# Sample attention of a decoder step: fresh keys turned once, second values loaded early, later value rows issued by ScalarE

## The reference

```python
kv_ext = jnp.concatenate([zeros(w), buf, kv_new], axis=1)
idx = q_idx[:, None] - offs[None, :]
logits = einsum('bhtd,btnhd->bhtn', q, kg) * HEAD_DIM ** -0.5 + bias
p = exp(logits - max); o = einsum('bhtn,btnhd->bthd', p / sum(p), vg)
```

## Time and profile before

| what | value |
|---|---|
| median of 3 runs | 2270.28 us (2265.86 to 2270.36) |
| profiled execution, its own time | 2268.59 us |
| span of the profiled execution | 2266.8 us |
| mean granted TensorE clock | 0.992 of full |
| DMA | 305.62 MB, mean 135 GB/s |
| attention stage in the span | about 1660 to 1828 us |

### The profile page before, as it was taken

One profiled execution on the slowest core, in us unless ns is written; L12 is line 12 of the kernel. 1 busy time (PEld: TensorE's weight loads), 2 busy tenths in 40 slices (PEclk: granted clock), 3 DMA queues, 4 the chain that ended last, 5 costly groups with the idle time before them and its releaser, 6 DMA issues.

```text
span 2266.8 us, 41700 instructions
## 1 busy us (share of the span) xinstructions
PE 2223.2 (98%) x17660; PEld 2104.2 (93%) x17660; DVE 1620.5 (71%) x2151; ACT 891.4 (39%) x1183; POOL 136.7 (6%) x189
## 2 busy tenths in 40 slices
PE   7999999999999999999999999999999999999998
PEld 6999999987799999998889999999976789999998
DVE  7983995699789749943459956984444579947963
ACT  6431443222754314432235422443145565423442
POOL 0000000323010000011001000001001100000001
PEclk8999999999999999999999999999999999999999
DMA  5543443554244435423339443532759833233321
GB/s 157 159 152 106 156 157 86 170 134 136 72 149 154 123 100 167 149 83 104 120 115 306 156 124 119 173 88 78 219 163 287 235 112 93 76 95 97 90 77 55
DMA packets 372155, 305.62 MB, mean 135 GB/s; under 512 B 13861, under 2 KB 338477, under 8 KB 371113
## 3 DMA queue, kind: packets, MB, share of 16 engines
q1 hardware_dynamic: 365549, 232.06, 36.2%
q0 software_dynamic: 6464, 71.76, 9.2%
q10 hardware_dynamic: 12, 0.02, 0.0%
HBM read 284.45 MB, written 70.54 MB: 157 GB/s over the span
## 4 chain that ended last, share of the span: by engine, by line
PE 89%; DVE 6%; issue 2%; ACT 2%; DMA 1%; SPq 0%; DVEq 0%; ACTq 0%
PE ps L2062 34%; PE ps L2118 13%; PE ps L2120 13%; PE ps L2119 13%; PE ps L2526 2%; PE ps L2524 2%; PE ps L2525 2%; PE ps L2362 2%; PE ps L2571 1%; PE ps L2672 1%; PE ps L2613 1%; DVE blk L1543 1%; PE ps L2625 1%; PE ps L2662 1%; DVE hlS L1520 1%
## 5 line engine op out<-in xcount | busy, mean ns | idle before, releaser
L1066 ACT CAST hlS<-blk 128x1024 fp32r<-128x1024 f32 x176 | 184.2, 1053 | 206.0 <-PE ps L2120 169.1
L2062 PE MATMUL ps<-actH,oWA 128*128 128x288 f32 x1408 | 250.4, 296 | 0.0
L2062 PE MATMUL ps<-actH,oWB 128*128 128x288 f32 x1408 | 250.0, 296 | 0.0
L1687 DVE SCALAR_TENSOR_TENSOR cs<-ps,rstd 128x576 f32<-128x576 f32 x64 | 48.5, 758 | 246.9 <-PE ps L2062 246.9
L1520 DVE TENSOR_TENSOR hlS<-blk,hlS 128x1024 fp32r<-128x1024 f32 x176 | 213.7, 1217 | 2.4 <-ACT hlS L1066 2.4
L2118 PE MATMUL ps<-tM,hlA 128*128 128x288 f32 x704 | 212.3, 302 | 2.9 <-DVE hlA L1520 2.4
L2118 PE MATMUL ps<-tE,hlS 128*128 128x288 f32 x704 | 208.5, 296 | 4.1 <-DVE hlS L1520 4.1
L2062 PEld LDWEIGHTS ps<-actH,oWA 128*128 128x128 f32 x1408 | 209.0, 189 | 1.2 <-DVE cs L1582 0.7
L2062 PEld LDWEIGHTS ps<-actH,oWB 128*128 128x128 f32 x1408 | 208.8, 189 | 0.0
L2118 PE MATMUL ps<-tM,hlS 128*128 128x288 f32 x704 | 208.1, 296 | 0.0
L2119 PE MATMUL ps<-tM,hlA 128*128 128x288 f32 x704 | 208.0, 296 | 0.0
(11 more groups left out here) (315 smaller groups left out, 5375.8 us busy)
## 6 DMA issues: line engine op xcount, KB each, us to landing
blk<-in_ffn_w_in SPq DMA_DIRECT2D x352, 256.0 KB, 4.1
raws<-in_ffn_w_out SPq DMA_DIRECT2D x64, 704.0 KB, 4.7
out_kv_sample<-in_cache_kv_w POOLq DMA_DIRECT2D x8, 4064.0 KB, 16.2
out_kv_sample<-in_cache_kv_w POOLq DMA_DIRECT2D x8, 2016.0 KB, 8.8
wst<-in_conv_w_pw SPq DMA_DIRECT2D x24, 512.0 KB, 4.2
wst<-in_w_kv SPq DMA_DIRECT2D x24, 512.0 KB, 3.8
kc<-in_cache_kv_w SPq DMA_DIRECT2D x40, 256.0 KB, 8.8
kc<-in_cache_kv_w SPq DMA_DIRECT2D x8, 1024.0 KB, 7.6
```

What stands on the lines that cost most here:

```text
L1066: nc.scalar.copy(o, a).then_inc(S["f_h"], 1)
L1687: nc.vector.scalar_tensor_tensor(px[m % 2], pair(2 + m % 2), 0.5, rstd[:], ALU.mult, ALU.mult).then_inc(S["px_ready"], 1)
L2062: nx = nc.tensor.matmul(outs[t], a, b[:, t, :], start=start and first, stop=stop and b is xh and not first)
```

## The change

The fresh keys of all entries (192 rows) are loaded at once in two halves of 96 rows, turned in two turns before the loop (`kf`), copied to `kfT` by DVE and kept. Part 2 of an entry's keys is then one turn (`k0`) of four 128x128 transposes, one for each pair, copied by one ACT instruction of 512 columns. The short score products read `kfT`. The sample probabilities are widened to ten full blocks, with zeros behind the fresh columns; the value products read 128 rows in the last block, of which POOL has set the unused ones to zero, and DVE copies the last two blocks at once. The second pair's values are loaded in the q stage. The seven value DMAs of entries 2 to 7 are issued by ACT at the end of its step, behind the same wait as before. Scratch buffers are placed anew, and the tiles `sbias` and `vinB` lie elsewhere. The diff, cut to its core (DVE's and ACT's loops skip part 2 alike; the placement of the tiles, the new semaphores, and the slices `sS[:, 0:SC]` are left out):

```diff
@@ -49,6 +49,8 @@
 SC = CN + 3 * NT
+SW = CN + P
+FR = 3 * SMP // 2
@@ -233,11 +235,13 @@
-    order = [(("kp", 0, g), "act") for g in range(3)]
+    order = [(("kp", 0, g), "act") for g in range(3)] + [(("kf", h), "dve") for h in range(2)]
...
         ks = sample_keys_of(s)
-        if ks:
+        if ks and ks[1] < 2:
             order += [(("ks", *ks, j), "dve" if j == 2 else "act") for j in range(PAIRS)]
+        elif ks:
+            order.append((("k0", ks[0]), "act"))
@@ -437,9 +445,9 @@
     def new_rows(t):
-        return t[0:24].rearrange("p a b -> p (a b)")[:, 0:AW]
-    kn, vn = new_rows(ta), (new_rows(tb), new_rows(rstd))
+        return t[:].rearrange("p a b -> p (a b)")[:, 0:AW]
+    kf, vn = (new_rows(ta)[0:FR], vcB[0:FR, 8, :]), (new_rows(tb), new_rows(rstd))
@@ -537,6 +545,27 @@
         return tM[:, :, p, low, :], hM[:, m]
+    c512 = I["cache_kv_w512"].rearrange("b (k p) v h d -> b p k v (h d)", p=P)
+    c128 = I["cache_kv_w128"].rearrange("b p v h d -> b p v (h d)")
+    c2048 = I["cache_kv_w2048"].rearrange("b (k m t) v h d -> b k m t v (h d)", k=4, t=16)
+    def value_rows(b, x, engine):
+        sem = S[f"vc_in{b % 2}"]
+        if x == 0:
+            engine.dma_start(vc[b % 2][:, 0:4, :], c512[b, :, :, 1, :]).then_inc(sem, 16)
+        elif x == 1:
+            for k in range(4):
+                engine.dma_start(vc[b % 2][:, 4 + k, :], c2048[b, k, :, 0:NT, 1, :]).then_inc(sem, 16)
+        else:
+            engine.dma_start(vc[b % 2][:, 8, :], c128[b, :, 1, :]).then_inc(sem, 16)
+    def fresh_values(b, engine):
+        r0 = (SEQ + NT * b) * 3
+        if b < 2:
+            engine.wait_ge(S["vn_void"], b + 1)
+        engine.dma_start(vn[b % 2][0:24], kvs3[r0:r0 + 24, AW:2 * AW]).then_inc(S[f"vc_in{b % 2}"], 16)
@@ -739,13 +768,11 @@
-        c512 = I["cache_kv_w512"].rearrange("b (k p) v h d -> b p k v (h d)", p=P)
-        c128 = I["cache_kv_w128"].rearrange("b p v h d -> b p v (h d)")
-        c2048 = I["cache_kv_w2048"].rearrange("b (k m t) v h d -> b k m t v (h d)", k=4, t=16)
-        def fresh(dst, b, kv, sem):
-            r0 = (SEQ + NT * b) * 3
-            sp.dma_start(dst, kvs3[r0:r0 + 24, kv * AW:(kv + 1) * AW]).then_inc(sem, 16)
+        def fresh_keys():
+            for h in range(2):
+                r0 = SEQ * 3 + FR * h
+                sp.dma_start(kf[h], kvs3[r0:r0 + FR, 0:AW]).then_inc(S["kf_in"], 16)
@@ -756,19 +783,6 @@
                 sp.dma_start(kc[:, 8, :], c128[b, :, 0, :]).then_inc(S["kc_in2"], 16)
-                fresh(kn, b, 0, S["kc_in2"])
-        def value_rows(b, x):
-            sem = S[f"vc_in{b % 2}"]
-            if x == 0:
-                sp.dma_start(vc[b % 2][:, 0:4, :], c512[b, :, :, 1, :]).then_inc(sem, 16)
-            elif x == 1:
-                for k in range(4):
-                    sp.dma_start(vc[b % 2][:, 4 + k, :], c2048[b, k, :, 0:NT, 1, :]).then_inc(sem, 16)
-            else:
-                sp.dma_start(vc[b % 2][:, 8, :], c128[b, :, 1, :]).then_inc(sem, 16)
-                fresh(vn[b % 2], b, 1, sem)
@@ -780,27 +794,32 @@
                 key_rows(0, c - 5)
+                if c == 7:
+                    fresh_keys()
             elif c < 11:
-                value_rows(0, c - 8)
+                value_rows(0, c - 8, sp)
             else:
-                value_rows(1, 0)
-        value_rows(1, 1)
+                value_rows(1, 0, sp)
+        value_rows(1, 1, sp)
+        pair_values(1)
...
         sp.dma_start(sbias[:], sbd).then_inc(S["sbias_in"], 16)
+        fresh_values(0, sp)
...
             if after and after[0] + 1 < NB:
-                sp.wait_ge(S["t_mm"], TURN["ks", *after, PAIRS - 1][0] + 1)
+                last = ("ks", *after, PAIRS - 1) if after[1] < 2 else ("k0", after[0])
+                sp.wait_ge(S["t_mm"], TURN[last][0] + 1)
...
                 pair_bias(1)
-                value_rows(1, 2)
-            elif s == 2:
-                pair_values(1)
+                sp.wait_ge(S["t_mm"], TURN["kf", 1][0] + 1)
+                value_rows(1, 2, sp)
+                fresh_values(1, sp)
@@ -811,10 +830,6 @@
                 pair_values((s - 3) // 6 + 2)
-            if s >= 3 and sample_unit(s - 3) is not None and sample_unit(s - 3) + 2 < NB:
-                sp.wait_ge(S["pv_mm"], s - 3 + 1)
-                for x in range(3):
-                    value_rows(sample_unit(s - 3) + 2, x)
@@ -945,6 +960,9 @@
         squares("q")
+        pool.wait_ge(S["evac"], MB["q"] + 12 + 4)
+        for t in vn:
+            nc.gpsimd.memset(t, 0.0).then_inc(S["vn_void"], 1)
@@ -1361,9 +1379,15 @@
             q, _, _ = TURN["ks", e, x, j]
-            a, n = ((C1, 512), (C2, 512), (C0, SC - C0))[x]
+            a = (C1, C2)[x]
             act.wait_ge(S["t_mm"], q + 1)
-            nc.scalar.copy(kTs[:, j, a:a + n], turned(("ks", e, x, j))[:, 0:n]).then_inc(S["t_act"], 1)
+            nc.scalar.copy(kTs[:, j, a:a + 512], turned(("ks", e, x, j))).then_inc(S["t_act"], 1)
+        def keys_dense(e):
+            act.wait_ge(S["t_mm"], TURN["k0", e][0] + 1)
+            nc.scalar.copy(kTs[:, :, C0:CN], turned(("k0", e)).rearrange("p (j n) -> p j n", j=PAIRS)
+                           ).then_inc(S["t_act"], 1)
@@ -1395,6 +1421,11 @@
                                ).then_inc(S["t_act"], 1)
+            if s >= 3 and sample_unit(s - 3) is not None and sample_unit(s - 3) + 2 < NB:
+                act.wait_ge(S["pv_mm"], s - 3 + 1)
+                for x in range(3):
+                    value_rows(sample_unit(s - 3) + 2, x, act)
+                fresh_values(sample_unit(s - 3) + 2, act)
@@ -1964,9 +1996,16 @@
-            a, n = ((C1, 512), (C2, 512), (C0, SC - C0))[x]
+            a = (C1, C2)[x]
             dve.wait_ge(S["t_mm"], TURN["ks", e, x, j][0] + 1)
-            nc.vector.tensor_copy(kTs[:, j, a:a + n], turned(("ks", e, x, j))[:, 0:n]).then_inc(S["t_dve"], 1)
+            nc.vector.tensor_copy(kTs[:, j, a:a + 512], turned(("ks", e, x, j))).then_inc(S["t_dve"], 1)
+        def keys_fresh(h):
+            dve.wait_ge(S["t_mm"], TURN["kf", h][0] + 1)
+            nc.vector.tensor_copy(kfT[:, :, FR * h:FR * (h + 1)],
+                                  turned(("kf", h))[:, 0:PAIRS * FR].rearrange("p (j n) -> p j n", j=PAIRS)
+                                  ).then_inc(S["t_dve"], 1)
@@ -1976,8 +2015,8 @@
             else:
-                nc.vector.tensor_copy(pT[:, 8, :], src[:, 0:P])
-                nc.vector.tensor_copy(pT[0:24, 9, :], src[0:24, P:2 * P]).then_inc(S["t_dve"], 1)
+                nc.vector.tensor_copy(pT[:, 8:10, :].rearrange("p x n -> p (x n)"), src[:, 0:2 * P]
+                                      ).then_inc(S["t_dve"], 1)
@@ -2564,14 +2605,27 @@
             if j == 0:
-                pe.wait_ge(S[f"kc_in{x}"], (16, 64, 32)[x] * (e + 1))
+                pe.wait_ge(S[f"kc_in{x}"], (16, 64)[x] * (e + 1))
             out, cols = bank_for(("ks", e, x, j)), slice(j * P, (j + 1) * P)
-            if x < 2:
-                for k in range(4):
-                    nx = nc.tensor.transpose(out[:, k * P:(k + 1) * P], kc[:, 4 * x + k, cols], ident[:])
-            else:
-                nc.tensor.transpose(out[:, 0:P], kc[:, 8, cols], ident[:])
-                nx = nc.tensor.transpose(out[:, P:P + 24], kn[:, cols], ident[0:24, 0:24])
+            for k in range(4):
+                nx = nc.tensor.transpose(out[:, k * P:(k + 1) * P], kc[:, 4 * x + k, cols], ident[:])
+            nx.then_inc(S["t_mm"], 1)
+        def keys_dense(e):
+            pe.wait_ge(S["kc_in2"], 16 * (e + 1))
+            out = bank_for(("k0", e))
+            for j in range(PAIRS):
+                nx = nc.tensor.transpose(out[:, j * P:(j + 1) * P], kc[:, 8, j * P:(j + 1) * P], ident[:])
+            nx.then_inc(S["t_mm"], 1)
+        def keys_fresh(h):
+            if h == 0:
+                pe.wait_ge(S["kf_in"], 32)
+            out = bank_for(("kf", h))
+            for j in range(PAIRS):
+                nx = nc.tensor.transpose(out[:, j * FR:(j + 1) * FR], kf[h][:, j * P:(j + 1) * P], ident[0:FR, 0:FR])
@@ -2604,14 +2658,17 @@
                 pe.wait_ge(S["q_ready"], e + 1)
-                pe.wait_ge(S["t_dve"], TURN["ks", e, 2, 2][2])
-                pe.wait_ge(S["t_act"], TURN["ks", e, 2, 3][2])
-                for bank, g, a, b, c, step in (
-                        (0, 1, C1, C2, 0, 1), (1, 2, C2, C0, 0, 1), (2, 0, C0, CN, 0, 1),
-                        (2, 0, CN, SC, P, 3), (2, 1, CN + 1, SC, P + 1, 3), (2, 2, CN + 2, SC, P + 2, 3)):
+                pe.wait_ge(S["t_dve"], TURN["ks", e, 1, 2][2])
+                pe.wait_ge(S["t_act"], TURN["k0", e][2])
+                for bank, g, a, b in ((0, 1, C1, C2), (1, 2, C2, C0), (2, 0, C0, CN)):
                     for j in range(PAIRS):
-                        nx = nc.tensor.matmul(ps[32 * j:32 * j + 32, bank, c:c + b - a:step], qs[:, 4 * g + j, :],
```

(39 more changed lines are left out.)

## The result

| | before | changed |
|---|---|---|
| median | 2268.66 us (2265.86 to 2272.19, 6 runs) | 2280.37 us (2276.30 to 2285.81, 6 runs) |
| profiled execution, its own time | 2268.59 us | 2279.97 us |
| span | 2266.8 us | 2278.1 us |

The ratio is 1.0049, with a 95% interval of 1.0039 to 1.0059. The changed kernel is slower by 11.1 us (8.9 to 13.4). The forecast was 2283.4 us, +14.8 us on the profiled execution; that one moved by +11.4 us.

A forecast was written before the change was run, and what follows sets the result against it. TensorE's stream in its written order was taken to bound the attention stage. Terms -8.5 -1.0 -0.5 +0.8 +19.0 +5.0 = +14.8 us on 2268.6 gave 2283.4 us; own range 2276 to 2291, with rivals 8 in 10 for 2259 to 2292.

The forecast's parts named there:

- What bounds the stage: Attention stage: TensorE's stream in written order bounds it; work taken from it counts in full; no time of its own.
- Parts 1 and 2: TensorE's window-128 key turns, four full transposes per entry, -8.5 us; value products with a full tenth block, -1.0 us.
- Part 3: Start of the attention stage: new fresh-key turns delay first scores, one ACT copy fewer; +0.8 us, from 0 to 1.2.
- Part 4: Seven DMA issues on ACT ahead of exp, six entries: each block stops TensorE for its length less 1.3 us; +19.0 us.
- my low end: Lower bound for one block of seven issues on ACT: 3.97 us less 0.48 us under the probability copy, 3.5 us.
- Part 5: TensorE's clock falls behind stops in the attention stage: four falls at 1.25 us each, +5.0 us.
- The key wait: TensorE's one wait for keys in the attention stage goes, as SyncE is freer ahead of key loads; -0.5 us.
- Silent gaps: TensorE's 2.86 us gap without a releaser in the trace: if it went, up to 4 us would go too.
- (1): Issues on ACT cost TensorE nothing and the kernel ends faster, at 2259.4 us; chance 0.20.
- (2): Short issue blocks on ACT, six shifts of 3.5 us, stops of 2.2 us, no clock loss: 2272.6 us; chance 0.15.
- (3): ACT and SyncE hinder each other; ACT pays SyncE's 33.7 us of issues, with six clock drops: 2292.8 us; chance 0.13.

The follow-up runs named there:

- the issues alone: Kernel before with one part of the change alone: ACT issues the seven value DMAs of entries 2 to 7 in one block; 2290.64 us, ratio 1.0090.
- the spread run: Changed kernel with the same seven issues on ACT, spread over its idle places instead of standing in one block; 2261.83 us, ratio 0.9963.
- the run with exp's table ahead: Changed kernel with the seven issues spread over ACT's idle places and exp's table loaded by ACT ahead of the attention stage; 2259.14 us, ratio 0.9959.

## Why the prediction was right, point by point

- **What bounds the stage:** TensorE's stream in its order. Right; where nothing disturbs it, work taken from it comes back in full.
- **Parts 1 and 2, -8.5 and -1.0 us:** worked out as 1.33 us a period. Measured in pure periods 1.38 us (19.13 to 17.75 us). Right. With part 3 the three terms sum to 8.7 us, and the stage without value rows shrank by 8.5 us.
- **Part 3, +0.8 us:** ACT's first prompt key copy to the first sample scores went from 10.58 us (1660.48 to 1671.06) to 11.46 us (1660.70 to 1672.16), +0.88 us. Right, and ACT's chain was what ended the wait: without the table load it was 1.34 us shorter. The first prompt scores came later than I said, at 1664.85 and not near 1664.4, but ACT's chain covered that.
- **Part 4, +19.0 us:** six stops at the place named, 17.6 us from start to start (16.7 us of idle time). The mechanism was right, shown from both sides (the issues alone: 16.1 us of idle time; without them: none). The term was too large by 1.4 us, and the step was the overlap: I had the 0.48 us under the probability copy in my low end but not in the 4.0 us of the sum, and each of the six blocks starts with that copy, 2.9 us in all. The slack was 1.3 us, as read: a shift of exp by 4.39 us delayed the fourth key turn by 3.06 us, one of 4.23 us by 2.89. The other way went the blocks, 28.2 us in sum for my 26.8: only one was as short as I had taken for four (4.05 us), and the two beside SyncE's prompt keys weren't much longer (4.82 and 5.02 us beside 4.65, 4.71 and 4.90).
- **Part 5, +5.0 us:** four falls of the clock, as counted. In three of those periods TensorE was busy for 1.4 to 1.5 us longer than in a like period with a stop at full clock (twice 19.38 us for 17.87, once 20.04 for 18.64), so the price is a little low. But the count was luck: the second profile of the same kernel has three falls. So was the choice: I gave the falls to the long stops, and a stop of 2.15 us had one while one of 2.91 us had none.
- **The key wait, -0.5 us:** gone in the changed kernel. That SyncE's freedom is the reason isn't shown: with SyncE free in the same way, the keys were late for 2.5 us in the spread run and not at all in the run with exp's table ahead. Of the five runs with value rows in which ACT stopped TensorE little or not at all, four had key waits, 2.5 to 5.4 us. What the prediction left out is what a stream that runs 7% faster asks of DMA engines at a share of 1.09; it priced that at nothing. In the changed kernel itself this didn't show, since the stops left time for the keys.
- **Silent gaps:** I had left them at 4.5 us and named the chance that they move. The profiled run had 1.7 us. That is -2.8 us, the largest part of the difference of 3.4 us between forecast and profile. The fall of the clock behind the long gap of the earlier trace rows, priced at 1.25 us, went too: behind the gap of 1.75 us in the changed kernel the clock stayed at 1.00 (1761.90 to 1765.90).
- **The rivals.** (1), issues at no cost, is out for this place and right for others: spread over ACT's idle time they cost nothing that can be measured. (2), short blocks, had the overlap right, the blocks too short (shifts of 3.6 to 4.6 us for its 3.5) and the clock wrong. (3), two issuers in each other's way: the blocks were 28.2 us in sum and not 33.7, so ACT didn't pay all that SyncE had paid. One issue of fresh rows took 1.09 us instead of 0.40 at a time when SyncE issued nothing, so the trace doesn't show a lock between the two as the cause of that length; what is, stays open.

## What to carry to other kernels

An issue moved to another engine takes that engine's time at that spot: read the slack where the instructions go, from the copy that another engine waits for, not from the engine's idle share. The same seven issues stopped TensorE for 17.6 us in one block with 1.3 us of slack, and cost nothing that could be measured when they were cut to fit ACT's idle places. And where the DMA engines are full, price what a faster stream asks of them: here four of the five faster runs with value rows waited 2.5 to 5.4 us for keys, the kernel before 0.5 us.

## What the runs showed of the hardware that I had not expected

- ACT's DMA issue starts together with the copy ahead of it (both at 1698.02, and within 0.01 us in all six blocks), where exp before started 0.48 us behind it. So the first 0.48 us of a block behind a 512-column copy are free.
- The silent gaps of TensorE, which nothing in the trace ends, hang on the traffic. Every profile that loaded the value rows had some (4.5 us before, 1.7 us changed, 0.6 us with the issues alone, 1.2 to 4.1 us in the others), and the two without them had none. What is late in the gaps, the traces don't name.
- Stops of 2.15 to 3.18 us on TensorE were followed by a fall of the granted clock in four of six cases in one execution and in three of six in another, without regard to which was longer. In the first of them the clock was 0.60 in 1748 to 1752 behind the stop of 3.11 us, and 1.00 in 1703 to 1707 around the one of 2.91 us.
